# Moving the buffers of a transformer kernel to other addresses in the on-chip memory

## The chip, the cores and the metric

The kernel runs on one core of a Trainium2 chip. The metric is the device time of one execution in microseconds (us), as the median over runs. A core has a matrix engine (TensorE, PE in the rows below, with its weight loads shown apart as PEld), a vector engine (VectorE, DVE), a scalar engine (ScalarE, ACT), a general engine (GpSimd, POOL) and queues that start DMA transfers (SyncE, SP). All of them work on one on-chip memory (SBUF) of 128 partitions; an address in this text is a byte offset inside a partition, the same in all of them.

## The reference, cut to what matters

Two transformer blocks in float32 run one after the other over a sequence of 512 tokens of width 1024. Every block has two layers, and every layer is a mixer (causal pooling, dilated attention, or retention beside stick-breaking attention) and a gated feed-forward part of width 2816.

```python
h = _modulate(_rmsnorm(x, norm2_g[layer]), sh2, sc2)
a, v = jnp.split(h @ w_up, 2, axis=-1)          # 1024 x 5632
a = _causal_dwconv(a, conv_w, conv_b)
x = x + g2[:, None, :] * ((jax.nn.silu(a) * v) @ w_down)   # 2816 x 1024
...
h = rms_norm(x, norm2_g[l])
x = x + (jax.nn.silu(h @ w_gate[l]) * (h @ w_up[l])) @ w_down[l]
```

## The kernel before, in words

Activations are held transposed, 128 channels by 512 tokens to a chunk, and every float32 product is made from three products of a reduced format (fp32r): each operand is split in a high and a low part, and high x high, high x low and low x high are added up in PSUM. `three` (L435) issues these three matmuls, all through `mm` (L432, the call on L433). Each has 128x128 weights (512 bytes of a partition) and streams one chunk of 512 columns (2048 bytes of a partition) past them. A step of `gemm` (L441) does this for 8 or 11 chunks.

The weights come from one long array in DRAM, `stream`. `load` (L1781) of the SP queue brings a unit of one or two tiles, mostly 1 MB, into one of two buffers `RAW`, or, for the modulation weights of the first stages, into one of three buffers `AR`. ScalarE copies a tile from `RAW` to one of three buffers `WH`, which rounds it to the high half (`prep`, through L821). GpSimd (first 79 tiles, L1687) or VectorE (all others, L1234) subtracts that from `RAW` and writes the low half to one of three buffers `WL`. VectorE multiplies what is in `AR` with the condition vector (L1256).

The moving operands are pairs of a high and a low buffer. `H1H` and `H1L` hold the input of most projections. `PH`/`PL` (named H2Ha, H2La in the rows) hold the pooled values, `AH`/`AL` (H2Hb, H2Lb) the second input of the attention projections, `HH`/`HL` (H2Hc, H2Lc) the outputs of the second block's mixers, and `GH`/`GL` (GHa, GHb, GHd and GLa, GLb, GLd) the gated hidden values that the down projections read. `SPH`/`SPO` are a smaller pair, read with the weights `KR`.

There are 10,416 matmuls of 512 columns in fp32r: 6720 stream H1H or H1L, 48 H2Ha or H2La, 1152 H2Hb or H2Lb, 384 H2Hc or H2Lc, 1056 GHd or GLd, and 528 each GHa/GLa and GHb/GLb. The rest of the matrix engine's work is in plain float32 (norm sums, transposes, attention products).

All buffers are placed by hand: `at(name, offset, n)` in `Core.__init__` (L257) gives a buffer of n words its byte offset. Different stages put different buffers over the same bytes. Each matmul of `gemm` starts at a multiple of 512 bytes inside its weight buffer and a multiple of 2048 bytes inside its moving buffer, so the remainder of a buffer's offset by 256 is that of every operand read from it. Before the change this remainder is 128 for H1H, H1L, RAW, WH, WL, SS and SG, and 64 for the H2, GH and GL pairs, SPH, SPO, KR, Q, K, AA, OC, W and AR.

Of the kernel before, what the change touches and what calls it, by code (L numbers as in the profile page):

```python
# [7 lines left out]
F32R = mybir.dt.float32r  # L8
# [7 lines left out]
SLOT = 2048  # L16
WSLOT = HC * 128
# [76 lines left out]
NCOL = 0  # L94
# [154 lines left out]
class Core:  # L249


    def __init__(self, nc, stream, cd, colsd, xt, basd, attd, retd, out):
# [4 lines left out]
        def at(name, offset, n, dt=F32):  # L257
            return nc.alloc_sbuf_tensor_at(name, [128, n], dt, offset=offset)


        self.XT = at("XT", 1152, 4096)
        self.H1H, self.H1L = at("H1H", 17536, 4096, F32R), at("H1L", 33920, 4096, F32R)
        self.RAW = [at(f"RAW{i}", 50304 + 8192 * i, SLOT) for i in range(2)]
        self.WH = [at(f"WH{i}", 66688 + 5632 * i, WSLOT, F32R) for i in range(3)]
        self.WL = [at(f"WL{i}", 83584 + 5632 * i, WSLOT, F32R) for i in range(3)]
        self.SS, self.SG = at("SS", 100480, 512), at("SG", 102528, 512)
        self.CO = at("CO", 104576, NCOL)
        self.MOD, self.AB, self.KON = at("MOD", 106176, 112), at("AB", 106624, 40), at("KON", 106784, 2)
        self.BAS, self.ONE128 = at("BAS", 106816, 576), at("ONES", 109120, 128)
        self.PS = [nc.alloc_psum_tensor(f"PS{i}", [128, 512], F32) for i in range(8)]  # L270

        self.AR = [at("AR0", 109632, SLOT), at("AR1", 117824, SLOT), at("AR2", 126016, SLOT)]
        self.COND = at("COND", 134208, 1024)
        early = {"SQ": [at(f"SQ{i}a", 138304 + 2048 * i, 512) for i in range(2)], "R": at("Ra", 142400, 512),
                 "T": [at(f"T{i}a", 144448 + 2048 * i, 512) for i in range(3)],
                 "V": [at(f"V{i}a", 150592 + 2048 * i, 512) for i in range(4)]}
        self.PH, self.PL = at("H2Ha", 158784, 4096, F32R), at("H2La", 175168, 4096, F32R)
        self.PU = [at(f"U{i}", 191552 + 2112 * i, 528) for i in range(2)]
        self.PV = [[at(f"V{j}{i}", 195776 + 4224 * i + 2112 * j, 528) for j in range(2)] for i in range(2)]

        self.AH, self.AL = at("H2Hb", 109632, 4096, F32R), at("H2Lb", 126016, 4096, F32R)
        self.ATT = at("ATT", 142400, 1152)
        self.QT = [at(f"QT{i}", 147008 + 6144 * i, 1536) for i in range(2)]
        self.KT = [at(f"KT{i}", 159296 + 6144 * i, 1536) for i in range(2)]
        self.VV = [at(f"VV{i}", 171584 + 6144 * i, 1536) for i in range(2)]
        self.OT, self.VF, self.STAT = at("OT", 183872, 4096), at("VF", 200256, 512), at("STAT", 202304, 16)
        self.AT = [at(f"T{i}b", 208512 + 2048 * i, 512) for i in range(3)]
        self.AV = [at(f"V{i}b", 214656 + 2048 * i, 512) for i in range(4)]
        self.SB = [at("SB0", 202368, 1536), at("SB1", 208512, 1536)]
        self.PT = [at("PT0", 214656, 1536), at("PT1", 220800, 1536)]  # L290

        late = {"SQ": [at(f"SQ{i}q", 109632 + 2048 * i, 512) for i in range(2)], "R": at("Rc", 113728, 512),
                "T": [at(f"T{i}c", 115776 + 2048 * i, 512) for i in range(3)],
                "V": [at(f"V{i}c", 121920 + 2048 * i, 512) for i in range(4)]}
# [5 lines left out]
        self.Y = [[at(f"Ya{i}", 203840 + 2048 * i, 512) for i in range(2)],  # L300
                  [at(f"Yb{i}", 175168 + 2048 * i, 512) for i in range(2)]]
        self.SI = [[at(f"SIa{i}", 207936 + 2048 * i, 512) for i in range(2)],
                   [at(f"SIb{i}", 179264 + 2048 * i, 512) for i in range(2)]]
        gh, gl = at("GHd", 113728, 5632, F32R), at("GLd", 136256, 5632, F32R)
        si = [at(f"SId{i}", 162880 + 2048 * i, 512) for i in range(2)]
        self.GH += [gh, gh]
        self.GL += [gl, gl]
        self.SI += [si, si]

        self.HH, self.HL = at("H2Hc", 113728, 4096, F32R), at("H2Lc", 130112, 4096, F32R)  # L310
        self.RT = at("RT", 146496, 3072)
        self.Q = [at(f"Q{i}", 158784 + 2048 * i, 512) for i in range(3)]
        self.K = [at(f"K{i}", 164928 + 2048 * i, 512) for i in range(3)]
        self.G = [at(f"G{i}", 171072 + 2048 * i, 512) for i in range(2)]
        self.W = [at(f"W{i}", 175168 + 2048 * i, 512) for i in range(3)]
        self.VR = at("VR", 181312, 512)
        self.TMP = {"k": at("TMP0", 183360, 512), "q": at("TMP1", 185408, 512)}
        self.AA, self.SPL = at("AA", 187456, 1280), at("SPL", 192576, 1280)
        self.SPH, self.SPO = at("SPH", 197696, 1280, F32R), at("SPO", 202816, 1280, F32R)
        self.KR = at("KR", 207936, 256, F32R)  # L320
        self.OB = [at(f"OB{i}", 208960 + 2048 * i, 512) for i in range(2)]
        self.OC = [at(f"OC{i}", 213056 + 2048 * i, 512) for i in range(2)]

        self.ONES = self.ONE128[:, :]
        self.IDENT, self.STRICT, self.MEANS = self.BAS[:, 0:128], self.BAS[:, 384:512], self.BAS[:, 512:576]
# [1529 lines left out]
```

How the kernel before makes its waits and increments, by code:

```python
    def wait_ge(self, sem, value):  # L243
        if value > self.met.get(id(sem), 0):
            self.engine.wait_ge(sem, value)
            self.met[id(sem)] = value
# [181 lines left out]
    def vacate(b):  # L428
        if b in free:
            q.wait_ge(*free[b])
# [10 lines left out]
    def gemm(t, H, L, ready, freed, mid=None):  # L441
        b, n = BANK[t], UNITS[TILES[t][0]][2][TILES[t][1]][3]
        q.wait_ge(*c.low(t))
        vacate(b)
        for k in range(n):
            if mid and k in (2, 4):
                mid(k)
            if ready:
                q.wait_ge(*ready(k))
            ins = three(b, t, 128 * k, chunk(H, k), chunk(L, k), k == 0, k == n - 1)
        ins.then_inc(c.mm, 1)
        free[b] = freed
# [1 line left out]
    def group(t0, inputs, freed, order=tuple(range(8)), split=4, hook=None):  # L455
        for n, k in enumerate(order[:split]):
            for x in range(3):
                H, L, ready = inputs[x]
                if n == 0:
                    q.wait_ge(*c.low(t0 + x))
                    vacate(BANK[t0 + x])
                q.wait_ge(*ready(k))
                three(BANK[t0 + x], t0 + x, 128 * k, chunk(H, k), chunk(L, k), n == 0, False)
                if hook:
                    hook(3 * n + x)
        for x in range(3):
            H, L, ready = inputs[x]
            for k in order[split:]:
                q.wait_ge(*ready(k))
                ins = three(BANK[t0 + x], t0 + x, 128 * k, chunk(H, k), chunk(L, k), False, k == order[-1])
            ins.then_inc(c.mm, 1)
            free[BANK[t0 + x]] = freed[x]
```

## Time and profile before

| what | value |
|---|---|
| median of 3 runs | 2838.7 us (2837.08 to 2839.62) |
| profiled execution | 2840.38 us, of which its span 2838.6 us |
| PE busy | 2723.9 us (96% of the span) |
| DVE, ACT, POOL busy | 1523.9, 1062.1, 388.6 us |
| granted TensorE clock, mean | 0.984 |
| DMA | 297.19 MB, mean 105 GB/s |

The span runs from the first to the last instruction of the core; what lies around it is 1.8 us here. Busy time of PE counts a stretch in which matmuls overlap once, so a busy PE is not a PE at its peak; how far apart two matmuls start is read from the rows of the timeline.

### The profile page before, as it was taken

The page shows a single profiled execution, that of the slowest core. Times are in us where ns is not written, and L with a number is a line of the kernel's source. Part 1 is how long each engine was busy: PE and PEld are TensorE (multiplying, and loading weights), DVE is VectorE, ACT ScalarE, POOL GpSimd, SP SyncE. Part 2 cuts the span into 40 slices and gives each one's busy share as a digit, 9 for nine tenths or more (in the row PEclk, how much of TensorE's full clock was granted, in tenths as well). Part 3 has the DMA queues.
Part 4 walks back from the last instruction along what each step waited for, and adds up shares of the span by engine and source line. Part 5 has one row for each costly group of instructions (what it writes and reads, how often), then busy time and mean ns, then how long its engine had stood idle before and what let it go on. Part 6 is the DMA issues. An engine that isn't in the chain of part 4 may idle for free.

```text
span 2838.6 us, 30758 instructions
## 1 busy us (share of the span) xinstructions
PE 2723.9 (96%) x12742; PEld 2186.1 (77%) x12742; DVE 1523.9 (54%) x2035; ACT 1062.1 (37%) x1488; POOL 388.6 (14%) x196
## 2 busy tenths in 40 slices
PE   5689999989999999899999999999999999999998
PEld 3568888778888887688888777788887777788886
DVE  7888857655555555654345555443344455443343
ACT  3333233344444444343234455422223455422231
POOL 3444545410000000000000001010010011010010
PEclk9799999999999999999999999999999999999999
DMA  7354645321212111122222221222223212223222
GB/s 271 119 210 183 248 177 198 135 83 60 75 61 74 69 66 60 60 89 101 95 89 102 97 75 60 76 102 97 89 95 113 90 60 75 76 103 101 85 100 71
DMA packets 45690, 297.19 MB, mean 105 GB/s; under 512 B 4976, under 2 KB 5104, under 8 KB 16368
## 3 DMA queue, kind: packets, MB, share of 16 engines
q1 hardware_dynamic: 45408, 294.71, 28.6%
q8 instruction: 101, 1.65, 0.2%
q10 hardware_dynamic: 144, 0.52, 0.1%
q14 instruction: 37, 0.30, 0.0%
HBM read 293.12 MB, written 2.10 MB: 104 GB/s over the span
## 4 chain that ended last, share of the span: by engine, by line
PE 89%; DVE 3%; ACT 1%; issue 1%; POOL 0%; DVEq 0%; ACTq 0%; POOLq 0%
PE PS L433 87%; PE PS L478 2%; DVE XT L1237 0%; DVE H2Lb L1234 0%; DVE WL L1234 0%; ACT H1H L821 0%; DVE AA L1234 0%; DVE H1L L1234 0%; DVE AR L1256 0%; ACT WH L821 0%; DVE T0c L1234 0%; DVE T1a L1234 0%; DVE T1c L1234 0%; ACT AA L821 0%; DVE T0a L1234 0%
## 5 line engine op out<-in xcount | busy, mean ns | idle before, releaser
L433 PE MATMUL PS<-H1H,WH 128*128 128x512 f32 x2240 | 898.2, 401 | 39.0 <-DVE H1L L1234 32.5
L433 PE MATMUL PS<-H1H,WL 128*128 128x512 f32 x2240 | 878.6, 392 | 0.0
L433 PE MATMUL PS<-H1L,WH 128*128 128x512 f32 x2240 | 877.8, 392 | 0.0
L1234 DVE TENSOR_TENSOR WL<-RAW,WH 128x1024 fp32r<-128x1024 f32 (+1 forms) x330 | 435.2, 1320 | 381.4 <-ACT WH L821 380.5
L821 ACT ACTIVATE WH<-RAW 128x1024 fp32r<-128x1024 f32 (+2 forms) x409 | 449.9, 1102 | 268.5 <-PE PS L433 257.7
L433 PEld LDWEIGHTS PS<-H1H,WH 128*128 128x128 f32 x2240 | 424.2, 189 | 143.6 <-issue 44.7
L433 PEld LDWEIGHTS PS<-H1L,WH 128*128 128x128 f32 x2240 | 424.8, 190 | 90.5 <-issue 5.3
L433 PEld LDWEIGHTS PS<-H1H,WL 128*128 128x128 f32 x2240 | 423.9, 189 | 91.0
L1687 POOL TENSOR_TENSOR WL<-RAW,WH 128x1024 fp32r<-128x1024 f32 (+2 forms) x79 | 229.8, 2914 | 235.8 <-ACT WH L821 235.6
L1256 DVE CUSTOM_DVE_ANT_0 AR<-AR,COND,CO 128x1024 f32<-128x1024 f32 x112 | 237.3, 2161 | 0.4
L433 PE MATMUL PS<-H2Hb,WH 128*128 128x512 f32 x384 | 160.0, 417 | 11.5 <-DVE H2Lb L1234 11.5
L433 PE MATMUL PS<-H2Lb,WH 128*128 128x512 f32 x384 | 152.6, 397 | 0.0
L433 PE MATMUL PS<-H2Hb,WL 128*128 128x512 f32 x384 | 152.6, 397 | 0.0
L1687 POOL TENSOR_TENSOR SId<-SId,SG 128x512 f32<-128x512 f32 x44 | 57.3, 1302 | 668.5 <-ACT SId L821 668.5
L433 PE MATMUL PS<-GHd,WL 128*128 128x512 f32 x352 | 138.7, 394 | 0.0
L433 PE MATMUL PS<-GHd,WH 128*128 128x512 f32 x352 | 138.7, 394 | 0.0
L433 PE MATMUL PS<-GLd,WH 128*128 128x512 f32 x352 | 138.7, 394 | 0.0
L1687 POOL TENSOR_TENSOR TMP<-TMP,RT 128x512 f32<-128x512 f32 x16 | 20.7, 1294 | 772.6 <-ACT TMP L821 772.6
L821 ACT ACTIVATE SB<-SB,STAT 128x768 f32<-128x768 f32 x64 | 60.0, 938 | 125.7 <-DVE STAT L1485 124.6
L1234 DVE TENSOR_TENSOR XT<-PS,XT 128x512 f32<-128x512 f32 x48 | 33.1, 689 | 128.8 <-PE PS L433 128.7
L433 PEld LDWEIGHTS PS<-H2Hb,WH 128*128 128x128 f32 x384 | 72.7, 189 | 31.8 <-DVE H2Lb L1234 7.9
L821 ACT ACTIVATE GHd<-SId 128x512 fp32r<-128x512 f32 x44 | 27.8, 633 | 168.3 <-DVE SId L1234 168.3
(246 smaller groups left out, 3334.3 us busy)
## 6 DMA issues: line engine op xcount, KB each, us to landing
RAW<-stream SPq DMA_DIRECT2D x170, 1024.0 KB, 4.8
AR<-stream SPq DMA_DIRECT2D x56, 1024.0 KB, 6.9
RAW<-stream SPq DMA_DIRECT2D x64, 704.0 KB, 4.0
RT<-ret SPq DMA_DIRECT2D x2, 1536.0 KB, 6.3
RAW<-stream SPq DMA_DIRECT2D x4, 640.0 KB, 6.9
XT<-xt SPq DMA_DIRECT2D x2, 1024.0 KB, 8.9
y<-XT SPq DMA_DIRECT2D x8, 256.0 KB, 2.5
ATT<-att SPq DMA_DIRECT2D x1, 576.0 KB, 3.4
```

Source lines behind the costliest of these rows:

```text
L433: return nc.tensor.matmul(out, weights, moving, start=start, stop=stop, skip_group_check=True)
L478: ins = nc.tensor.transpose(PS[b][:, 128 * n:128 * n + 128], block, c.IDENT)
L821: return nc.scalar.activation(out, src, fn, **kw)
L1234: return nc.vector.tensor_tensor(out, a, b, op)
L1256: ins = nc.vector.tensor_tensor_reduce(src, src, c.COND[:, :], 1.0, bias, ALU.mult, ALU.add, c.mod(first + n, 1))
L1687: return nc.gpsimd.tensor_tensor(out, a, b, op)
```

## The change

The diff gives nearly every buffer another offset. No instruction, loop, wait or size is touched. After it the remainder by 256 is 0 for H1H, H1L, RAW, WH, WL, SS, SG and CO, for all H2, GH and GL pairs, SPH, SPO, KR, Q, K, W, AA, OB, OC and the buffers QT, KT and VV of the attention. It stays 64 for AR, COND, BAS and ONES (110400, the offset of AR0, is 431.25 x 256) and becomes 64 for SB and PT, and 128 for Yb and SIb. XT keeps its offset, with the remainder 128. MOD, AB and KON move down into the gap behind XT. Gaps of 256 or 512 bytes are left between some buffers, as between H1H and H1L.

```diff
         self.XT = at("XT", 1152, 4096)
-        self.H1H, self.H1L = at("H1H", 17536, 4096, F32R), at("H1L", 33920, 4096, F32R)
-        self.RAW = [at(f"RAW{i}", 50304 + 8192 * i, SLOT) for i in range(2)]
-        self.WH = [at(f"WH{i}", 66688 + 5632 * i, WSLOT, F32R) for i in range(3)]
-        self.WL = [at(f"WL{i}", 83584 + 5632 * i, WSLOT, F32R) for i in range(3)]
+        self.MOD, self.AB, self.KON = at("MOD", 17536, 112), at("AB", 17984, 40), at("KON", 18144, 2)
+        self.H1H, self.H1L = at("H1H", 18432, 4096, F32R), at("H1L", 35072, 4096, F32R)
+        self.RAW = [at(f"RAW{i}", 51456 + 8192 * i, SLOT) for i in range(2)]
+        self.WH = [at(f"WH{i}", 68096 + 5632 * i, WSLOT, F32R) for i in range(3)]
+        self.WL = [at(f"WL{i}", 84992 + 5632 * i, WSLOT, F32R) for i in range(3)]
...
-        self.AR = [at("AR0", 109632, SLOT), at("AR1", 117824, SLOT), at("AR2", 126016, SLOT)]
+        self.AR = [at(f"AR{i}", 110400 + 8192 * i, SLOT) for i in range(3)]
...
-        self.PH, self.PL = at("H2Ha", 158784, 4096, F32R), at("H2La", 175168, 4096, F32R)
+        self.PH, self.PL = at("H2Ha", 159744, 4096, F32R), at("H2La", 176128, 4096, F32R)
...
-        self.AH, self.AL = at("H2Hb", 109632, 4096, F32R), at("H2Lb", 126016, 4096, F32R)
+        self.AH, self.AL = at("H2Hb", 110592, 4096, F32R), at("H2Lb", 127488, 4096, F32R)
...
-        self.GH = [at("GHa", 158784, 5632, F32R), at("GHb", 130112, 5632, F32R)]
-        self.GL = [at("GLa", 181312, 5632, F32R), at("GLb", 152640, 5632, F32R)]
+        self.GH = [at("GHa", 160768, 5632, F32R), at("GHb", 131328, 5632, F32R)]
+        self.GL = [at("GLa", 183808, 5632, F32R), at("GLb", 153856, 5632, F32R)]
...
-        gh, gl = at("GHd", 113728, 5632, F32R), at("GLd", 136256, 5632, F32R)
+        gh, gl = at("GHd", 114688, 5632, F32R), at("GLd", 139264, 5632, F32R)
...
-        self.HH, self.HL = at("H2Hc", 113728, 4096, F32R), at("H2Lc", 130112, 4096, F32R)
+        self.HH, self.HL = at("H2Hc", 115456, 4096, F32R), at("H2Lc", 132096, 4096, F32R)
...
-        self.SPH, self.SPO = at("SPH", 197696, 1280, F32R), at("SPO", 202816, 1280, F32R)
-        self.KR = at("KR", 207936, 256, F32R)
+        self.SPH, self.SPO = at("SPH", 199680, 1280, F32R), at("SPO", 204800, 1280, F32R)
+        self.KR = at("KR", 209920, 256, F32R)
```

## Rows read from the trace of the kernel before

**Rows 1.** The page: busy time, and the chain that ended last.

```profile
PE 2723.9 (96%) x12742; PEld 2186.1 (77%) x12742; DVE 1523.9 (54%) x2035; ACT 1062.1 (37%) x1488; POOL 388.6 (14%) x196
...
PE 89%; DVE 3%; ACT 1%; issue 1%; POOL 0%; DVEq 0%; ACTq 0%; POOLq 0%
```

**Rows 2.** Windows: the head, the first feed-forward stage, its densest stretch, all after it.

```profile
core 0: us, PE busy (x) PEld busy (x) DVE busy (x) ACT busy (x) POOL busy (x), PEclk, DMA share, GB/s
...
300.00:350.00 50.00, 50.00 (x217) 40.32 (x216) 44.76 (x39) 13.09 (x12) 27.07 (x9) 1.00 0.72 270
0.00:200.00 200.00, 133.54 (x486) 101.33 (x486) 160.97 (x208) 64.86 (x84) 81.00 (x43) 0.87 0.51 200
200.00:556.00 356.00, 354.69 (x1543) 289.07 (x1543) 254.89 (x254) 114.63 (x136) 172.90 (x59) 1.00 0.52 195
...
1584.00:2838.60 1254.60, 1235.50 (x5368) 988.11 (x5366) 577.55 (x756) 469.60 (x658) 107.68 (x78) 0.99 0.24 85
```

**Rows 3.** Timeline of PE, H1H and H1L streamed: first and last of 55 matmuls.

```profile
start us, us, engine line op out<-in xcount [idle before <-releaser]
1299.75 0.39 PE L433 MATMUL PS<-H1H,WL 128*128 128x512 f32 x1
...
1311.99 0.39 PE L433 MATMUL PS<-H1H,WL 128*128 128x512 f32 x1
```

**Rows 4.** Timeline of PE, GHb and GLb streamed: first and last of 43 matmuls.

```profile
1503.04 0.39 PE L433 MATMUL PS<-GHb,WH 128*128 128x512 f32 x1
...
1512.84 0.39 PE L433 MATMUL PS<-GHb,WH 128*128 128x512 f32 x1
```

**Rows 5.** Timeline of PE, H2Hb and H2Lb streamed: first and last of 12 matmuls.

```profile
632.96 0.39 PE L433 MATMUL PS<-H2Hb,WH 128*128 128x512 f32 x1
...
635.53 0.40 PE L433 MATMUL PS<-H2Hb,WL 128*128 128x512 f32 x1
```

**Rows 6.** Timeline of PE at half clock, H1H and H1L: 7 matmuls.

```profile
26.68 0.63 PE L433 MATMUL PS<-H1L,WH 128*128 128x512 f32 x1
...
29.24 0.63 PE L433 MATMUL PS<-H1L,WH 128*128 128x512 f32 x1
```

**Rows 7.** Timeline of PE, plain float32: 8 matmuls, 2560 columns together, and the next.

```profile
1778.40 2.39 PE L433 MATMUL PS<-Q,K 128*128 128x512 f32 x8 [0.78 <-ACT OB L821]
1780.55 0.48 PE L433 MATMUL PS<-H2Hc,WH 128*128 128x512 f32 x1
```

**Rows 8.** Timeline of PE, SPH and SPO on KR: first of 8 (2560 columns), and the next.

```profile
1661.38 0.45 PE L433 MATMUL PS<-SPH,KR 128*128 128x512 f32 x1
...
1662.66 0.44 PE L433 MATMUL PS<-H1H,WH 128*128 128x512 f32 x1
```

**Rows 9.** Groups by line, PE, from 200 us on: one of each three kinds.

```profile
line engine op names shapes xcount | busy us, mean ns | idle before us <-releasers
L433 PE MATMUL PS<-H1H,WL 128*128 128x512 f32 x2097 | 819.7, 391 | 0.0
...
L433 PE MATMUL PS<-H2Lb,WH 128*128 128x512 f32 x384 | 152.6, 397 | 0.0
...
L433 PE MATMUL PS<-GHd,WL 128*128 128x512 f32 x352 | 138.7, 394 | 0.0
...
L433 PE MATMUL PS<-GHa,WL 128*128 128x512 f32 x176 | 69.3, 394 | 0.0
...
L433 PE MATMUL PS<-H2Hc,WH 128*128 128x512 f32 x128 | 53.1, 415 | 3.3 <-DVE WL L1234 2.0 <-DVE AA L1234 0.9
```

**Rows 10.** Waits of PE from 200 to 556 us.

```profile
PE PS L433 <- ACT SQ1a L821: 0.6, 1, 0.6
PE PS L433 <- POOL H1L L1687: 0.2, 1, 0.2
```

**Rows 11.** The page: the copy of a tile to WH with its waits, and the loads.

```profile
L821 ACT ACTIVATE WH<-RAW 128x1024 fp32r<-128x1024 f32 (+2 forms) x409 | 449.9, 1102 | 268.5 <-PE PS L433 257.7
...
RAW<-stream SPq DMA_DIRECT2D x170, 1024.0 KB, 4.8
```

More of the change, by code:

```diff
@@ L261, in __init__ @@
         self.XT = at("XT", 1152, 4096)
-        self.H1H, self.H1L = at("H1H", 17536, 4096, F32R), at("H1L", 33920, 4096, F32R)
-        self.RAW = [at(f"RAW{i}", 50304 + 8192 * i, SLOT) for i in range(2)]
-        self.WH = [at(f"WH{i}", 66688 + 5632 * i, WSLOT, F32R) for i in range(3)]
-        self.WL = [at(f"WL{i}", 83584 + 5632 * i, WSLOT, F32R) for i in range(3)]
-        self.SS, self.SG = at("SS", 100480, 512), at("SG", 102528, 512)
-        self.CO = at("CO", 104576, NCOL)
-        self.MOD, self.AB, self.KON = at("MOD", 106176, 112), at("AB", 106624, 40), at("KON", 106784, 2)
@@ L269, in __init__ @@
-        self.BAS, self.ONE128 = at("BAS", 106816, 576), at("ONES", 109120, 128)
-        self.PS = [nc.alloc_psum_tensor(f"PS{i}", [128, 512], F32) for i in range(8)]
-        self.AR = [at("AR0", 109632, SLOT), at("AR1", 117824, SLOT), at("AR2", 126016, SLOT)]
[L273 to L276, printed above, removed]
@@ L277, in __init__ @@
-        self.PH, self.PL = at("H2Ha", 158784, 4096, F32R), at("H2La", 175168, 4096, F32R)
-        self.PU = [at(f"U{i}", 191552 + 2112 * i, 528) for i in range(2)]
-        self.PV = [[at(f"V{j}{i}", 195776 + 4224 * i + 2112 * j, 528) for j in range(2)] for i in range(2)]
-        self.AH, self.AL = at("H2Hb", 109632, 4096, F32R), at("H2Lb", 126016, 4096, F32R)
-        self.ATT = at("ATT", 142400, 1152)
-        self.QT = [at(f"QT{i}", 147008 + 6144 * i, 1536) for i in range(2)]
-        self.KT = [at(f"KT{i}", 159296 + 6144 * i, 1536) for i in range(2)]
@@ L285, in __init__ @@
[L285 to L294, printed above, removed]
@@ L296, in __init__ @@
-        self.NORM = [early] * 3 + [late] * 6
-        self.GH = [at("GHa", 158784, 5632, F32R), at("GHb", 130112, 5632, F32R)]
-        self.GL = [at("GLa", 181312, 5632, F32R), at("GLb", 152640, 5632, F32R)]
[L300 to L303, printed above, removed]
@@ L304, in __init__ @@
-        gh, gl = at("GHd", 113728, 5632, F32R), at("GLd", 136256, 5632, F32R)
-        si = [at(f"SId{i}", 162880 + 2048 * i, 512) for i in range(2)]
+        self.MOD, self.AB, self.KON = at("MOD", 17536, 112), at("AB", 17984, 40), at("KON", 18144, 2)
+        self.H1H, self.H1L = at("H1H", 18432, 4096, F32R), at("H1L", 35072, 4096, F32R)
+        self.RAW = [at(f"RAW{i}", 51456 + 8192 * i, SLOT) for i in range(2)]
+        self.WH = [at(f"WH{i}", 68096 + 5632 * i, WSLOT, F32R) for i in range(3)]
@@ new lines, in __init__ @@
+        self.WL = [at(f"WL{i}", 84992 + 5632 * i, WSLOT, F32R) for i in range(3)]
+        self.SS, self.SG = at("SS", 101888, 512), at("SG", 103936, 512)
+        self.CO = at("CO", 105984, NCOL)
+        self.BAS, self.ONE128 = at("BAS", 107584, 576), at("ONES", 109888, 128)
+        self.PS = [nc.alloc_psum_tensor(f"PS{i}", [128, 512], F32) for i in range(8)]
+        self.AR = [at(f"AR{i}", 110400 + 8192 * i, SLOT) for i in range(3)]
+        self.COND = at("COND", 134976, 1024)
+        early = {"SQ": [at(f"SQ{i}a", 139072 + 2048 * i, 512) for i in range(2)], "R": at("Ra", 143168, 512),
+                 "T": [at(f"T{i}a", 145216 + 2048 * i, 512) for i in range(3)],
+                 "V": [at(f"V{i}a", 151360 + 2048 * i, 512) for i in range(4)]}
@@ new lines, in __init__ @@
+        self.PH, self.PL = at("H2Ha", 159744, 4096, F32R), at("H2La", 176128, 4096, F32R)
+        self.PU = [at(f"U{i}", 192512 + 2112 * i, 528) for i in range(2)]
+        self.PV = [[at(f"V{j}{i}", 196736 + 4224 * i + 2112 * j, 528) for j in range(2)] for i in range(2)]
+        self.AH, self.AL = at("H2Hb", 110592, 4096, F32R), at("H2Lb", 127488, 4096, F32R)
+        self.ATT = at("ATT", 143872, 1152)
+        self.QT = [at(f"QT{i}", 148480 + 6144 * i, 1536) for i in range(2)]
+        self.KT = [at(f"KT{i}", 160768 + 6144 * i, 1536) for i in range(2)]
@@ new lines, in __init__ @@
+        self.VV = [at(f"VV{i}", 173056 + 6144 * i, 1536) for i in range(2)]
+        self.OT, self.VF, self.STAT = at("OT", 185344, 4096), at("VF", 201728, 512), at("STAT", 203776, 16)
+        self.AT = [at(f"T{i}b", 209984 + 2048 * i, 512) for i in range(3)]
+        self.AV = [at(f"V{i}b", 216128 + 2048 * i, 512) for i in range(4)]
+        self.SB = [at("SB0", 203840, 1536), at("SB1", 209984, 1536)]
+        self.PT = [at("PT0", 216128, 1536), at("PT1", 222272, 1536)]
+        late = {"SQ": [at(f"SQ{i}q", 110592 + 2048 * i, 512) for i in range(2)], "R": at("Rc", 114688, 512),
+                "T": [at(f"T{i}c", 116736 + 2048 * i, 512) for i in range(3)],
+                "V": [at(f"V{i}c", 122880 + 2048 * i, 512) for i in range(4)]}
@@ new lines, in __init__ @@
+        self.NORM = [early] * 3 + [late] * 6
+        self.GH = [at("GHa", 160768, 5632, F32R), at("GHb", 131328, 5632, F32R)]
+        self.GL = [at("GLa", 183808, 5632, F32R), at("GLb", 153856, 5632, F32R)]
+        self.Y = [[at(f"Ya{i}", 206336 + 2048 * i, 512) for i in range(2)],
+                  [at(f"Yb{i}", 176512 + 2048 * i, 512) for i in range(2)]]
+        self.SI = [[at(f"SIa{i}", 210432 + 2048 * i, 512) for i in range(2)],
+                   [at(f"SIb{i}", 180608 + 2048 * i, 512) for i in range(2)]]
@@ L306, in __init__ @@
+        gh, gl = at("GHd", 114688, 5632, F32R), at("GLd", 139264, 5632, F32R)
+        si = [at(f"SId{i}", 161792 + 2048 * i, 512) for i in range(2)]
         self.GH += [gh, gh]
@@ L308, in __init__ @@
         self.SI += [si, si]
-        self.HH, self.HL = at("H2Hc", 113728, 4096, F32R), at("H2Lc", 130112, 4096, F32R)
[L311 to L318, printed above, removed]
-        self.SPH, self.SPO = at("SPH", 197696, 1280, F32R), at("SPO", 202816, 1280, F32R)
-        self.KR = at("KR", 207936, 256, F32R)
-        self.OB = [at(f"OB{i}", 208960 + 2048 * i, 512) for i in range(2)]
-        self.OC = [at(f"OC{i}", 213056 + 2048 * i, 512) for i in range(2)]
+        self.HH, self.HL = at("H2Hc", 115456, 4096, F32R), at("H2Lc", 132096, 4096, F32R)
+        self.RT = at("RT", 148480, 3072)
+        self.Q = [at(f"Q{i}", 160768 + 2048 * i, 512) for i in range(3)]
+        self.K = [at(f"K{i}", 166912 + 2048 * i, 512) for i in range(3)]
+        self.G = [at(f"G{i}", 173056 + 2048 * i, 512) for i in range(2)]
+        self.W = [at(f"W{i}", 177152 + 2048 * i, 512) for i in range(3)]
+        self.VR = at("VR", 183296, 512)
+        self.TMP = {"k": at("TMP0", 185344, 512), "q": at("TMP1", 187392, 512)}
+        self.AA, self.SPL = at("AA", 189440, 1280), at("SPL", 194560, 1280)
+        self.SPH, self.SPO = at("SPH", 199680, 1280, F32R), at("SPO", 204800, 1280, F32R)
+        self.KR = at("KR", 209920, 256, F32R)
+        self.OB = [at(f"OB{i}", 210944 + 2048 * i, 512) for i in range(2)]
+        self.OC = [at(f"OC{i}", 215040 + 2048 * i, 512) for i in range(2)]
         self.ONES = self.ONE128[:, :]
```

## The prediction

> **What bounds the kernel now.** I read the page's busy times and chain first. The matrix engine is busy 96% of the span and makes up 89% of the chain that ended last [rows 1]. The windows say where: until 200 us it is busy 133.5 of 200 us, at a mean clock of 0.87, while VectorE is busy 161; from 200 to 556 us it is busy 354.7 of 356 [rows 2] and waits 0.8 us in all [rows 10]; from 1584 us it is busy 98.5%. So from 200 us on the time is the number of matmuls times the distance between their starts, and a change of addresses matters if it alters that distance. In the head it would be worth little, since VectorE sets the pace there.
>
> Next I read that distance in the timeline, and this is what decides. The rows print 0.01 us, so I divide long stretches. With H1H and H1L streamed, 54 distances take 12.24 us, 226.7 ns each [rows 3]. With GHb and GLb, 42 take 9.80 us, 233.3 ns [rows 4]. With H2Hb and H2Lb, 11 take 2.57 us, 233.6 ns [rows 5], which I take as 233.3. The shape, the weight buffers and the full clock are the same. At half clock, 1.2 GHz, 6 distances with H1H take 2.56 us, 426.7 ns [rows 6]: 512 columns at one a cycle and nothing more. At full clock, 2.4 GHz, the columns alone would take 213.3 ns. So at full clock each matmul carries an excess, 13.3 ns over H1 and 20.0 over the others.
>
> What differs between the two? Not the stage: H1 and H2Hb tiles alternate within the attention stage. Not the distance between high and low buffer: it is 16384 bytes for H1 and for H2Hb both. What differs is the offset's remainder by 256, 128 for H1 and 64 for all others. The excess looks like an effect of address, of a kind that shows only when operands are read at full rate.
>
> **The change part by part.** No instruction, wait or transfer is added or removed; every cost is in what an access takes at its new address.
>
> *The matmuls.* The two excesses are 32 and 48 columns' time, and (256 - remainder)/4 is 32 and 48: as if the reader went to the end of the 256-byte block in which an operand ends, and began the next only then. At remainder 0 the operand ends with its block and this excess is gone. What is left then is a fixed cost per matmul, which plain float32 shows because its slower rate hides the other part: 8 matmuls with 2560 columns take 2.15 us against 2.133 us at 1.2 columns a ns, 2.1 ns each [rows 7]. I take 213.3 + 2.1 = 215.4 ns. The bounds for the distance at remainder 0: from below 213.3 ns, the columns alone; from above 240.0 ns, if 0 counts as a whole block more (64 columns, the line 233.3, 226.7 carried one step the wrong way). I take the lower side, since it needs no extra read.
>
> The counts from 200 us on, where each kind of row stands for three of equal count: 3 x 2097 = 6291 over H1, and 3 x (384 + 352 + 176 + 176 + 128) = 3648 over the others [rows 9]; the second 176 is GHb, whose three rows equal GHa's.
> - H1: 6291 x (226.7 - 215.4 = 11.3 ns) = 71.1 us
> - others: 3648 x (233.3 - 215.4 = 17.9 ns) = 65.3 us
> - SPH and SPO: 8 matmuls over 2560 columns take 1.28 us where the columns are 1.07 us [rows 8]. There are 160; even 12 ns each is 2 us, and I count 1.
> - Taken off: the stretches at half clock after 200 us, where the excess is already hidden. The clock of 0.99 to 1.00 there [rows 2] leaves by estimate 60 matmuls, 1 us.
>
> *The rest of the load on the other engines.* With a matrix engine 6% faster the others must keep up. The tightest place is 300 to 350 us: VectorE 44.8, POOL 27.1 of 50 us, DMA share 0.72 [rows 2]. Six percent more makes that 47.5, 28.7 and 0.76. VectorE has 2.5 us in 50 left; the cover is thin, and over the whole 356 us it has 101 us to spare. I charge 2 us for new waits; if VectorE held half of that gain in this stage it would be 10 us. After 556 us VectorE is busy below 55%.
>
> *The streamed buffers.* A load of 1 MB lands in 4.8 us, and one unit of two tiles is needed per 48 x 0.227 = 10.9 us; ScalarE's copy to WH waits mostly for the matrix engine (257.7 of 268.5 us) [rows 11]. Faster or slower landing is worth nothing while this slack of 6 us stands. AR stays at remainder 64, so VectorE's multiplication, which sets the head, changes nothing: 0, at most 3 us either way. For ScalarE, VectorE and GpSimd I have no row that tells addresses apart, and outside the head they hide under matmuls: 0.
>
> *Sum.* 71.1 + 65.3 + 1 - 1 - 2 = 134 us. Against this execution, 2838.6 + 1.8 us around the span = 2840.4, that gives 2706; it stands 1.7 us above the median, so against the median 2838.7 - 134 = **2705 us**.
>
> *A rule on the other side.* The trace shows 426.7 ns at half and 226.7 or 233.3 ns at full clock, all with operands that start at multiples of 64 bytes [rows 3, 4, 6]. The Trainium skill, SBUF — State Buffer, section Specifications (TRN2), gives the memory lines of 16 bytes, with full bandwidth for an access that stays in a line; by that grain all these operands were aligned before, and the sum would be 0. The two distances differ all the same, so this trace doesn't bear the 16-byte grain out as the only one.
>
> **The rivals.**
> - *Only the step from 64 to 128 bytes counts* (a grain of 128 bytes, or only the place of the moving operand against its weights, which is equal for H1 before and for all after). Then 13.3 ns stay, say as the price of the weight load beside the stream, and the others fall to 226.7: 3648 x 6.67 ns = 24 us, 2814 us. For it: each remainder is seen once, and weights always at 128. Against: with both at 64, SPH and SPO on KR show (1.28 - 1.07)/8 = 27 ns each, more than 13.3 [rows 8], though these change bank often and the number is rough.
> - *A step of 64 bytes at each level.* 233.3, 226.7 and then 220.0 (6.67 ns is 16 columns, 64 bytes). 6291 x 6.67 + 3648 x 13.3 ns = 42 + 49 = 91 us, 2748 us. It also covers a smaller part of the excess left by weight loads.
> - *Remainder 0 is the worst, not the best.* If a block is read beyond the end also when the operand ends on it, the distance is 240.0: 6291 x 13.3 + 3648 x 6.67 ns = 84 + 24 = 108 us more, 2947 us. It decides as soon as the distance over H1 is above 226.7 by more than the others fall below 233.3 (in the ratio 3648 to 6291, 0.58). For it: the pattern alone, 48 then 32, doesn't tell 0 from 64. Against: it makes the even address dearer than any other.
> - *The map does nothing.* Something that I haven't seen sets the two distances, and the time stays at 2839. Against: the three GH pairs, at other places and in other stages, all show 394 ns for the length of a matmul without an interruption, and H1 391 [rows 9]; and the alternation of H1 and H2Hb in one stage excludes most other causes.
>
> On the weight load the Trainium skill, TensorE: Matmul & The Clock Gate, section Step-by-step, says that the engine has two independent read ports, so that loading the next weights takes nothing from the running matmul. No run here shows it; it speaks against the first rival's way to keep 13.3 ns. The same page, Back-to-back issue gap, has N/2.4 + 2.5 ns without a term for the address, 215.8 ns for 512 columns; the trace's 226.7 and 233.3 disagree with it.
>
> **How the numbers follow.** The full effect, near 2705: 0.47. The 64-byte step, near 2748: 0.12. Only 64 to 128, near 2814: 0.20. Nothing: 0.08. Worst at 0, near 2947: 0.10, and 0.03 for a slowdown by another way. The forecast's own range goes from 2838.7 - (6291 x 13.3 + 3648 x 20.0 ns = 157 us) = 2682 to about 2720, with 10 us of new waits and some distances that don't settle. The range for 8 in 10 starts at 2678 (the 157 us, and up to 4 more from the head and from SPH and SPO) and takes in the first two rivals up to 2822. Within 0.2% of the time before, about 6 us, is what a measurement of this kernel can't tell from no change. Faster 0.79, same 0.08, slower 0.13.
>
> **What would show it.** In the timeline the distance over H1H and over GHb becomes the same, 215 to 216 ns, and the mean of the uninterrupted kinds falls by as much as the distance. The distance at half clock stays 426.7. 200 to 556 us shrinks by some 5%, the head stays near 200 us, and VectorE's busy time is unchanged. The prediction is wrong if H1's distance stays at 226.7 or rises, or if waits of the matrix engine for VectorE appear between 200 and 556 us.

## The result, and the profile after

| | median, us | runs | ratio to before (95% interval) | span of the profiled execution, us |
|---|---|---|---|---|
| before | 2839.16 | 2837.08 to 2840.28 (4) | | 2838.6 |
| after | 2819.19 | 2819.10 to 2819.76 (4) | 0.9931 (0.9914 to 0.9948) | 2817.4 |

The new map is faster by 20 us, 0.7%. The forecast had 134 us; the range held the time only because it took in the first rival (2814 us), and that is the one which came true in size.

The page of the kernel after, busy times, answers to [rows 1]: PE lost 19.9 us of busy time with the same 12742 matmuls, and DVE and ACT lost under 1 us each.

```profile
PE 2704.0 (96%) x12742; PEld 2188.8 (78%) x12742; DVE 1523.1 (54%) x2035; ACT 1061.6 (38%) x1488; POOL 386.6 (14%) x196
...
RAW<-stream SPq DMA_DIRECT2D x170, 1024.0 KB, 4.7
```

The windows of after, same stretches as [rows 2] (columns there):

```profile
0.00:200.00 200.00, 134.80 (x490) 102.72 (x491) 162.22 (x210) 64.84 (x85) 81.73 (x43) 0.87 0.51 200
200.00:556.00 356.00, 350.37 (x1541) 288.89 (x1540) 257.83 (x258) 118.37 (x141) 172.19 (x60) 1.00 0.52 195
300.00:350.00 50.00, 50.00 (x223) 41.39 (x222) 46.17 (x41) 11.95 (x11) 27.44 (x9) 1.00 0.78 288
```

Clock and head are as before. From 300 to 350 us PE starts 223 matmuls where it started 217, and still waits for nobody. From 200 to 556 us it is idle for 5.6 us: 5.0 of them is one wait for DVE behind the stage, which comes before 556 us now; before, the same wait of 5.1 us came just after 556 us.

Now the distance between starts, PE's timeline of after. First H1H and H1L streamed (first and last of 70 matmuls), then GHb and GLb (76), then SPH and SPO on KR with the next matmul behind them:

```profile
1296.05 0.39 PE L433 MATMUL PS<-H1H,WL 128*128 128x512 f32 x1
...
1311.69 0.39 PE L433 MATMUL PS<-H1H,WL 128*128 128x512 f32 x1
...
1492.80 0.39 PE L433 MATMUL PS<-GHb,WH 128*128 128x512 f32 x1
...
1509.80 0.39 PE L433 MATMUL PS<-GHb,WH 128*128 128x512 f32 x1
...
1649.31 0.45 PE L433 MATMUL PS<-SPH,KR 128*128 128x512 f32 x1
1649.60 0.39 PE L433 MATMUL PS<-SPO,KR 128*128 128x512 f32 x1
...
1650.48 0.27 PE L433 MATMUL PS<-SPO,KR 128*128 128x128 f32 x1
1650.59 0.45 PE L433 MATMUL PS<-H1H,WH 128*128 128x512 f32 x1
```

69 distances over H1 take 15.64 us, 226.7 ns, exactly what [rows 3] had. 75 over GHb take 17.00 us, 226.7 ns, where [rows 4] had 233.3. SPH and SPO take 1.28 us as before [rows 8]; 0.29 of it is the first of the eight distances and 0.11 the last, and the six between, 1920 columns, take 0.88 us, 13.3 ns each above their columns. So H1 gained nothing and the others 6.67 ns each. The groups by line of after, from 200 us on, say the same of every matmul, against [rows 9]:

```profile
L433 PE MATMUL PS<-H1H,WL 128*128 128x512 f32 x2096 | 818.8, 391 | 0.0
L433 PE MATMUL PS<-H2Hb,WL 128*128 128x512 f32 x384 | 151.5, 395 | 0.0
...
L433 PE MATMUL PS<-GHd,WL 128*128 128x512 f32 x352 | 136.9, 389 | 0.0
...
L433 PE MATMUL PS<-GHa,WL 128*128 128x512 f32 x176 | 68.5, 389 | 0.0
...
L433 PE MATMUL PS<-H2Hc,WH 128*128 128x512 f32 x128 | 52.6, 411 | 3.5 <-DVE WL L1234 2.1 <-DVE AA L1234 1.0 <-DVE H2Lc L1234 0.5
```

H1 stays at 391 ns, GHd and GHa fall from 394 to 389, H2 by 2 to 4.

**Where the 21.2 us of span went.** I measured each stage between the starts of its first matmul and of the next stage's, in both traces. The eight down projections, 264 matmuls each over GH and GL, went from 61.6 to 59.8 us: 1.76 us, which is 264 x 6.67 ns, and 14.1 in all. The attention stage went from 638.9 to 635.2 us (3.75), the two mixers lost 1.05 us each, the head 1.2 (not traced further); the stages that stream H1 alone are within 0.05 us. Together 21.2. Attention gave half of its 1152 x 6.67 ns = 7.7 us, because there H2 is streamed in short stretches. In after a stretch doesn't begin at 226.7. PE's timeline, H2Hb behind an interruption, up to the next one:

```profile
637.79 0.48 PE L433 MATMUL PS<-H2Hb,WH 128*128 128x512 f32 x1
638.11 0.39 PE L433 MATMUL PS<-H2Lb,WH 128*128 128x512 f32 x1
...
639.04 0.40 PE L433 MATMUL PS<-H2Hb,WL 128*128 128x512 f32 x1
639.28 0.60 PE L478 MATMUL PS<-BAS,SB 128*128 128x128 f32 x4
```

From 638.11 to 639.04 four distances take 0.93 us, 232 ns. Farther on in a long stretch it is 226 (from 627.84 to 629.65 us, 8 distances).

The mean over all stretches of the trace that begin with H2Hb (88 of them, fewer reach the later places) shows how it settles: 232.7, 231.9, 230.2 and 229.6 ns for the first four distances of after, 227.0 for the tenth. In the trace of before, with the other addresses, the same stretches stay between 232.6 and 234.0 over the first ten. H1 settles in the same way in both traces. So at the start of a stretch the old and the new address cost nearly the same, and the 6.67 ns are saved only once the stream has run on for about ten matmuls.

### The profile page after: what moved, and what is told of

It is laid out like the page before. It is cut to its first block, busy times and chain, and to the rows that moved or that the text cites. A ratio compares the mean times of both kernels' runs of the same rounds, so it can differ in the third digit from the quotient of the medians.

```text
span 2817.4 us, 30758 instructions
## 1 busy us (share of the span) xinstructions
PE 2704.0 (96%) x12742; PEld 2188.8 (78%) x12742; DVE 1523.1 (54%) x2035; ACT 1061.6 (38%) x1488; POOL 386.6 (14%) x196
## 4 chain that ended last, share of the span: by engine, by line
PE 89%; DVE 3%; ACT 1%; issue 1%; DVEq 0%; POOL 0%; ACTq 0%; POOLq 0%
PE PS L433 87%; PE PS L478 2%; DVE H2Lb L1234 0%; DVE XT L1237 0%; DVE WL L1234 0%; DVE AA L1234 0%; ACT H1H L821 0%; DVE AR L1256 0%; DVE H1L L1234 0%; ACT WH L821 0%; DVE T1b L1234 0%; DVE T0c L1234 0%; DVE T1c L1234 0%; ACT AA L821 0%; ACT OC L821 0%
## 5 line engine op out<-in xcount | busy, mean ns | idle before, releaser
L1687 POOL TENSOR_TENSOR WL<-RAW,WH 128x1024 fp32r<-128x1024 f32 (+2 forms) x79 | 229.6, 2912 | 232.5 <-ACT WH L821 232.3
```

Source lines behind the costliest of these rows:

```text
L1687: return nc.gpsimd.tensor_tensor(out, a, b, op)
```

## The experiments

Two questions: does the remainder of an operand's own address count, or its place against the other operand's, and what are the 13.3 ns that stayed? Below, the *place* is the moving operand's offset less that of its weights, modulo 256 bytes, written from -96 to 128. Before it was 0 for H1 (128 and 128) and -64 for the others (64 and 128); for SPH and SPO on KR it was 0 as well (64 and 64). After it is 0 for all. That 256 bytes is the period and not 512 can be read from after: GHb and GLb lie 256 bytes off their weights modulo 512, GHa and GLa 0, and both take 226.7 ns.

**1. Shift only the upper part of the old map by 64 bytes.** Made from the kernel before, so that GH and H2 lie at remainder 128 with the weights; H1, RAW, WH and WL stay where they were, at 128.

```diff
-            return nc.alloc_sbuf_tensor_at(name, [128, n], dt, offset=offset)
+            return nc.alloc_sbuf_tensor_at(name, [128, n], dt, offset=offset + (64 if offset >= 109632 else 0))
```

> The kernel before with one part of the change alone: every buffer from 109632 on (H2, GH and GL pairs, AR, all stage buffers) moved up by 64 bytes, to the remainder 128, which H1, RAW, WH and WL already had. Relative theory (the distance between matmul starts hangs on the moving operand's remainder by 256 minus the weights'; equal gives 226.7 ns): all pairs fall from 233.3 to 226.7 ns, and the time is that of the changed kernel, about 2819 us. Grain theory (the moving operand wants a multiple of 128 bytes, whatever the weights have): the same, 2819. Theory that multiples of 256 bytes are needed, or that the streamed buffers' own alignment brought the gain: 2835 to 2839, as before.

Measured: 2818.64 us (2815.62 to 2820.05), ratio 0.9924 (0.9909 to 0.9939). The timeline and the groups from 200 us on:

```profile
1330.18 0.39 PE L433 MATMUL PS<-GHb,WL 128*128 128x512 f32 x1
...
1339.93 0.39 PE L433 MATMUL PS<-GHb,WH 128*128 128x512 f32 x1
...
L433 PE MATMUL PS<-GHd,WL 128*128 128x512 f32 x352 | 136.9, 389 | 0.0
```

43 distances take 9.75 us, 226.7 ns. One shift of 64 bytes has the whole gain. That H1, RAW and the weights go from remainder 128 to 0 adds nothing that these runs tell.

**2. Move only the weights of the new map.** Everything else at remainder 0, the weights at 64, 128 and 192.

```diff
-        self.WH = [at(f"WH{i}", 68096 + 5632 * i, WSLOT, F32R) for i in range(3)]
-        self.WL = [at(f"WL{i}", 84992 + 5632 * i, WSLOT, F32R) for i in range(3)]
+        # w64: 67904 and 84800; w128: 67968 and 84864; w192: 68032 and 84928
+        self.WH = [at(f"WH{i}", 67904 + 5632 * i, WSLOT, F32R) for i in range(3)]
+        self.WL = [at(f"WL{i}", 84800 + 5632 * i, WSLOT, F32R) for i in range(3)]
```

> The changed kernel with WH and WL moved down by 192 bytes to the remainder 64; all moving operands stay at 0. Relative theory: moving minus weights is -64 (192), as it was for GH and H2 before, so every one of the 9939 matmuls after 200 us goes from 226.7 to 233.3 ns, H1's too: 66 us more, 2885 us. Grain theory, or any in which only the moving operand's own address counts: no change, 226.7 ns and 2819 us.

> The changed kernel with WH and WL moved down by 128 bytes to the remainder 128; all moving operands at 0, so moving minus weights is 128. Relative theory: the distance is another than 226.7 ns; if each 64 bytes is worth 6.7 ns in one direction (-64 cost 6.7 more, so +64 gives 6.7 less), it is 213.3 to 215.4 or 240.0, thus about 2705 or 2950 us. Grain theory and own-address theories: 226.7 ns, 2819 us.

> The changed kernel with WH and WL moved down by 64 bytes to the remainder 192; moving minus weights is +64. Relative theory: if the effect has a direction, 220.0 ns and 2753 us; if it counts only how far apart they are, 233.3 ns as for -64, 2885 us. Grain theory and own-address theories: 226.7 ns, 2819 us.

| weights at | place | median, us | ratio to before (95% interval) | distance, ns |
|---|---|---|---|---|
| 64 | -64 | 2877.62 | 1.0132 (1.0115 to 1.0149) | 233.3 |
| 128 | 128 | 2869.73 | 1.0106 (1.0091 to 1.0121) | 233.4 |
| 192 | 64 | 2835.92 | 0.9988 (0.9978 to 0.9997) | 228.8 |

The timeline with the weights at 64 (first and last of 43 matmuls), and its group of H1; then the timeline with them at 128 (45) and at 192 (44):

```profile
1330.20 0.39 PE L433 MATMUL PS<-H1H,WH 128*128 128x512 f32 x1
...
1340.00 0.39 PE L433 MATMUL PS<-GHb,WH 128*128 128x512 f32 x1
...
L433 PE MATMUL PS<-H1H,WL 128*128 128x512 f32 x2098 | 830.6, 396 | 0.0
```

```profile
1329.68 0.40 PE L433 MATMUL PS<-H1H,WH 128*128 128x512 f32 x1
...
1339.95 0.40 PE L433 MATMUL PS<-GHb,WL 128*128 128x512 f32 x1
```

```profile
1330.03 0.39 PE L433 MATMUL PS<-GHb,WH 128*128 128x512 f32 x1
...
1339.87 0.39 PE L433 MATMUL PS<-GLb,WH 128*128 128x512 f32 x1
```

42 distances in 9.80 us are 233.3 ns, 44 in 10.27 are 233.4, 43 in 9.84 are 228.8. H1 never moved from 0 in these kernels and went from 391 to 396 ns a matmul: the moving operand's own remainder doesn't make its price. The weights' own remainder doesn't either, since at 128 they cost nothing in experiment 1 and 6.67 ns here. With the weights at 64, the old price now falls on H1 as well, 6291 x 6.67 = 42 us, against 38.5 measured over the kernel before. Between the weights at 64 and at 128 lie 8 us that the distances explain only in part: at 128 the last two down projections take 232.3 ns a matmul, the others 233.3.

**3. Three places in one kernel.** The three weight buffers take turns, each at its own remainder.

```diff
-        self.WH = [at(f"WH{i}", 68096 + 5632 * i, WSLOT, F32R) for i in range(3)]
-        self.WL = [at(f"WL{i}", 84992 + 5632 * i, WSLOT, F32R) for i in range(3)]
+        self.WH = [at(f"WH{i}", 67840 + 11264 * i + [32, 96, 160][i], WSLOT, F32R) for i in range(3)]
+        self.WL = [at(f"WL{i}", 73472 + 11264 * i + [32, 96, 160][i], WSLOT, F32R) for i in range(3)]
+        # mixb: [32, 192, 224] in both lines
```

> The changed kernel with the three pairs of weight buffers at the remainders 32, 96 and 160 (tiles 0, 1, 2 of every three), so moving minus weights is -32, -96 and +96; the distance is read tile by tile. Known from before and the runs so far: 0 gives 226.7 ns, -64 233.3, 128 233.4, +64 229.2. Smooth curve: -32 about 230, -96 about 233, +96 about 231, and no remainder below 226.7. [...] Time by the smooth curve: mean 231.3, 2819 + 9939 x 4.7 ns = 2865 us.

> The changed kernel with the three pairs of weight buffers at the remainders 32, 192 and 224, so moving minus weights is -32, +64 and +32. -32 must repeat what the run with 32, 96 and 160 shows and +64 the 229.2 ns of the run with all weights at 192. Smooth curve with its best place at 0: +32 about 228. If the best place lies between 0 and +64, +32 is below 226.7 ns, and all weights there would beat the changed kernel. Time about 2819 + 9939 x 1.7 ns = 2836 us by the smooth curve.

One run each: 2880.06 us (before, on that chip, 2840.28) and 2862.97 us. A tile of the down projection is 33 matmuls on one buffer. The boundaries of three in mixa, weights at 160 (place 96), 32 (-32), 96 (-96):

```profile
1336.97 0.40 PE L433 MATMUL PS<-GHb,WH 128*128 128x512 f32 x1
...
1344.67 0.40 PE L433 MATMUL PS<-GHb,WH 128*128 128x512 f32 x1
...
1352.38 0.39 PE L433 MATMUL PS<-GHb,WH 128*128 128x512 f32 x1
...
1360.10 0.40 PE L433 MATMUL PS<-GHb,WH 128*128 128x512 f32 x1
```

7.70, 7.71 and 7.72 us, so 233.3, 233.6 and 233.9 ns. In mixb the same reading gives 233.3 at 32, 233.3 at -32 and 229.1 at 64. A step of 64 bytes at each level would have given more than two values in order; instead there is 226.7 at 0, 229 at 64 and one plateau.

**4. Places under 64 bytes.** H1H and H1L moved up by 16 bytes, GHa and GLa down by 16, GHd and GLd up by 4. RAW and SId, which one of the copies reads, went up by 32.

```diff
-        self.H1H, self.H1L = at("H1H", 18432, 4096, F32R), at("H1L", 35072, 4096, F32R)
+        self.H1H, self.H1L = at("H1H", 18432, 4104, F32R)[:, 4:4100], at("H1L", 35072, 4104, F32R)[:, 4:4100]
...
-        self.GH = [at("GHa", 160768, 5632, F32R), at("GHb", 131328, 5632, F32R)]
-        self.GL = [at("GLa", 183808, 5632, F32R), at("GLb", 153856, 5632, F32R)]
+        self.GH = [at("GHa", 160736, 5640, F32R)[:, 4:5636], at("GHb", 131328, 5632, F32R)]
+        self.GL = [at("GLa", 183776, 5640, F32R)[:, 4:5636], at("GLb", 153856, 5632, F32R)]
...
-        gh, gl = at("GHd", 114688, 5632, F32R), at("GLd", 139264, 5632, F32R)
+        gh, gl = at("GHd", 114688, 5640, F32R)[:, 1:5633], at("GLd", 139264, 5640, F32R)[:, 1:5633]
```

> The changed kernel with small offsets of the moving operands against weights at 0: H1H and H1L +16 bytes, GHa and GLa -16, GHd and GLd +4, all others unchanged (so GHb and GLb must repeat 226.7 ns). The runs so far have 0 at 226.7, +64 at 229.1 and -32, +32, +96, 128 and -96 between 233.2 and 233.8. If what counts is that both lie on the same place within 256 bytes to the byte: +16, -16 and +4 are all near 233.3, 2819 + (6291 + 528 + 1056) x 6.7 ns = 2872 us. If the grain is 32 bytes: those that stay in the same 32 bytes as 0 (+16, +4) keep 226.7, or cost by the straddling alone. If the best place is near 0 but not at it, one of them is below 226.7.

One run: 2860.68 us (before 2839.01). Its groups from 200 us on, and the first and last matmul of the two down projections over GHa, 264 matmuls each:

```profile
L433 PE MATMUL PS<-H1H,WL 128*128 128x512 f32 x2096 | 828.0, 395 | 0.0
...
L433 PE MATMUL PS<-GHd,WL 128*128 128x512 f32 x344 | 137.8, 401 | 0.0
...
L433 PE MATMUL PS<-GHa,WL 128*128 128x512 f32 x176 | 69.9, 397 | 0.0
```

```profile
310.81 0.39 PE L433 MATMUL PS<-GHa,WH 128*128 128x512 f32 x1
...
373.02 0.40 PE L433 MATMUL PS<-GHa,WL 128*128 128x512 f32 x1
...
495.57 0.39 PE L433 MATMUL PS<-GHa,WH 128*128 128x512 f32 x1
...
556.94 0.39 PE L433 MATMUL PS<-GHa,WL 128*128 128x512 f32 x1
```

A length of 389 to 391 ns was 226.7 ns of distance, 396 was 233.3. Here 16 bytes up is 395 (231.6 in the timeline), 4 up 401, the worst of all (about 238). 16 down is 397, which is a mean of two values: 263 distances take 62.21 us in the first projection, 236.5 ns, and 61.37 in the second, 233.3, with the same buffers at the same place. So off place 0 the place alone doesn't fix the distance to the nanosecond. At place 0 all eight projections of after have 226.7, and no place tried beats it:

| place, bytes | -96 | -64 | -32 | -16 | 0 | 4 | 16 | 32 | 64 | 96 | 128 |
|---|---|---|---|---|---|---|---|---|---|---|---|
| distance, ns | 233.9 | 233.3 | 233.3 | 233.3 and 236.5 | 226.7 | 238 | 231.6 | 233.3 | 229 | 233.3 | 233.4 |

**5. What are the 13.3 ns: a smaller load.** If they are the weight load's reads, loading half as many weight columns must cut them. The two correction matmuls take 64 columns of their weights, and fill 64 rows of PSUM: the other 64 rows miss their correction.

```diff
-        mm(PS[b][:, :], wh, lo, False, False)
-        return mm(PS[b][:, :], wl, hi, False, last)
+        mm(PS[b][0:64, :], wh[:, 0:64], lo, False, False)
+        return mm(PS[b][0:64, :], wl[:, 0:64], hi, False, last)
```

> The changed kernel, but the two correction matmuls of every three (high weights by low input, low weights by high input) use only the first 64 of the 128 weight columns, so half of the outputs lack the corrections; it still streams 512 columns three times. Weight-load theory (the 13.3 ns that stay at full clock are the price of loading 128 columns of weights beside the stream): in two of three distances the load beside is half as long, 6.7 ns less each, triple mean 222.2 ns, 2775 us. Fixed-cost theory (13.3 ns belong to a 512-column fp32r stream whatever is loaded): 226.7 ns throughout, 2819 us.

> As the run with 64 weight columns in the correction matmuls, and WH and WL at the remainder 64 (moving minus weights -64). Weight-load theory: the whole 20 ns scale with the load, 10 in two of three distances, mean 226.7 ns, 2819 us. If only the placement part (6.7 ns) scales: 213.3 + 13.3 + 4.4 = 231 ns, 2863 us. If nothing scales: 233.3 ns, 2878 us.

2840.72 us with the weights at 0 and 2861.46 with them at 64, one run each (before, beside them, 2840.28). Neither theory: the smaller load made the kernel 21 us slower than after. Timeline, weights at 0, first and last of seven:

```profile
1330.11 0.39 PE L433 MATMUL PS<-GHb,WH 128*128 128x512 f32 x1
1330.33 0.39 PE L433 MATMUL PS<-GLb,WH 128*64 128x512 f32 x1
...
1331.48 0.39 PE L433 MATMUL PS<-GHb,WH 128*128 128x512 f32 x1
```

Six distances take 1.37 us, 228 ns, over longer stretches 229.5; the best place has lost part of its advantage. With the weights at 64 the mean is 231.6, less than 233.3, but not everywhere: the two projections over GHa stay at 233.3, the six over GHb and GHd go to 231.1, all at the same place. So the price isn't the load's width times a constant. That it depends on when, or over what length, the load's reads lie under the stream is argued, not shown: these matmuls also fill only half of their outputs.

**6. Fixed, or per column?** Each matmul split into two of 256 columns, each with its own weight load: twice as many matmuls, the same columns.

```diff
-        mm(PS[b][:, :], wh, hi, first, False)
-        mm(PS[b][:, :], wh, lo, False, False)
-        return mm(PS[b][:, :], wl, hi, False, last)
+        for n, (weights, moving) in enumerate(((wh, hi), (wh, lo), (wl, hi))):
+            for x in (0, 256):
+                ins = mm(PS[b][:, x:x + 256], weights, moving[:, x:x + 256], first and n + x == 0, last and n == 2)
+        return ins
```

> The changed kernel with every fp32r matmul of 512 columns issued as two of 256; the computation is the same, with twice as many weight loads. It asks what the 13.3 ns are that stay at full clock (226.7 against 213.3 ns). Fixed cost per matmul: 256 columns take 106.7 + 13.3 = 120 ns, 240 per 512 columns, 9939 x 13.3 ns = 132 us more, 2951 us. Cost per column streamed: 113.3 ns, no change, 2819 us. Weight load beside the stream: there are twice as many loads, as the fixed cost, or more, since a load has half as long to hide.

2940.72 us, in one run (before 2839.01). Timeline, two matmuls to a row:

```profile
1329.36 0.40 PE L433 MATMUL PS<-H1L,WH 128*128 128x256 f32 x2
...
1330.80 0.40 PE L433 MATMUL PS<-H1L,WH 128*128 128x256 f32 x2
```

12 distances take 1.44 us, 120.0 ns each: 106.7 for 256 columns, plus the same 13.3. It is a price per matmul with its load, not per column, as the six short distances of SPH and SPO also have it. The whole kernel pays 121.5 us over after, where 9939 x 13.3 ns would be 132.

**7. Another type.** First the two corrections alone took the upper halves of the same words as bfloat16 (their products are coarser).

```diff
+        def top(ap):
+            return ap.bitcast(mybir.dt.bfloat16).rearrange("p (n two) -> p n two", two=2)[:, :, 1]
...
-        mm(PS[b][:, :], wh, lo, False, False)
-        return mm(PS[b][:, :], wl, hi, False, last)
+        mm(PS[b][:, :], top(wh), top(lo), False, False)
+        return mm(PS[b][:, :], top(wl), top(hi), False, last)
```

> The changed kernel, but the two correction matmuls of every three read only the upper 16 bits of their float32 words, as bfloat16 with a step of 4 bytes, so the corrections are less precise; columns, addresses and footprint are the same, and half of the bytes count. If the 13.3 ns belong to reading 4-byte words at full rate, those two run at 216 ns and only the fp32r one keeps 226.7, mean 219, 2819 - 9939 x 7.6 ns = 2743 us. If they belong to the footprint or to the matmul as such: 226.7 ns, 2819 us.

2883.83 us in one run (before 2839.01). It doesn't answer its question, because the changes of type have a price of their own. Timeline:

```profile
1329.65 0.59 PE L433 MATMUL PS<-H1H,WH 128*128 128x512 f32 x1
1330.08 0.40 PE L433 MATMUL PS<-H1L,WH 128*128 128x512 bf16 x1
1330.32 0.39 PE L433 MATMUL PS<-H1H,WL 128*128 128x512 bf16 x1
1330.35 0.60 PE L433 MATMUL PS<-H1H,WH 128*128 128x512 f32 x1
```

The three starts lie 430, 240 and 30 ns apart, 700 for the triple, where three of one type take 680. So all three matmuls became bfloat16 (all products coarser), with the weight buffers at places 0, -64 and 64:

> The changed kernel with all three matmuls of every chunk reading only the upper 16 bits of their float32 words, as bfloat16 with a step of 4 bytes (coarser products, no change of data type between them), and with the three pairs of weight buffers at the remainders 0, 64 and 192, so moving minus weights is 0, -64 and +64 from tile to tile. If both the fixed 13.3 ns and the price of placement belong to fp32r: about 216 ns (213.3 and some 2 ns) in all three kinds of tile, 2819 - 9939 x 11 ns = 2710 us. If the fixed part is of any matmul with 512 columns from 4-byte steps: 226.7. If placement counts here too: tiles with the weights at 64 take longer than those at 0.

2797.8 us in one run (before 2840.63). The timeline at the boundaries of tiles of 33, with places 64, 0 and -64, and the weight loads' group:

```profile
1300.31 0.39 PE L433 MATMUL PS<-GHb,WH 128*128 128x512 bf16 x1
...
1307.75 0.39 PE L433 MATMUL PS<-GHb,WH 128*128 128x512 bf16 x1
...
1315.17 0.39 PE L433 MATMUL PS<-GHb,WH 128*128 128x512 bf16 x1
...
1322.65 0.39 PE L433 MATMUL PS<-GHb,WH 128*128 128x512 bf16 x1
...
L433 PEld LDWEIGHTS PS<-H1L,WH 128*128 128x128 bf16 x2240 | 217.8, 97 | 284.9 <-issue 13.6
```

7.44, 7.42 and 7.48 us: 225.5, 224.8 and 226.7 ns. The load lasts 97 ns instead of 190, and the distance at place 0 falls by under 2. So 11.5 ns of excess stay with another type and with a load half as long; neither float32r nor the length of the load makes up most of the 13.3. The spread over these three places is 1.9 ns where float32r has 6.67.

## Why the prediction was right in direction and wrong in size

**Right.** The matrix engine sets the time from 200 us on, through the distance between starts, and only its addresses matter. The two distances 226.7 and 233.3 are an effect of address: one shift of 64 bytes turns one into the other. At half clock it stays hidden, 426.7 ns after as before. The landing of RAW (4.7 for 4.8 us) and the busy times of DVE and ACT hardly moved, and the head by 1.2 us. The 2 us for new waits weren't needed: the one wait for DVE between 200 and 556 us is the 5 us that before had just behind them. The prediction's own first sign of being wrong came: H1's distance stayed at 226.7 ns.

**The step that failed** is this one: "At remainder 0 the operand ends with its block and this excess is gone. What is left then is a fixed cost per matmul, which plain float32 shows because its slower rate hides the other part". I had read both excesses, 13.3 and 20.0 ns, as one effect with two sizes, because (256 - remainder)/4 happens to be 32 and 48 columns. That was two points and a formula made for them, with the weights at one and the same remainder in both. They are two effects. 13.3 ns are paid per matmul whatever the map is: at 512 columns and at 256, with both operands at remainder 128 (before, experiment 1) or at 0 (after). The other 6.67 ns depend on the place of the moving operand against its weights. Plain float32's 2.1 ns, taken as what is fixed, were no measure of it: that row runs at 1.2 columns a ns, the rate of half clock, at which nothing of the excess shows in float32r either (426.7 ns).

Term by term: H1, forecast 71.1 us, measured 0, since its place was 0 before and after. The others, forecast 65.3 (3648 x 17.9 ns), measured 19.95 in the stages (14.1 + 3.75 + 2.1): 6.67 ns each in the down projections, about half of that in attention, where short stretches don't settle. "Some distances that don't settle" stood in the prediction's range, but at no price. SPH and SPO, forecast 1, measured 0.

**The rivals.** The first had two versions. Its "place of the moving operand against its weights" is what happened; its 24 us were 4 too many for attention and the mixers. Its other version, a grain of 128 bytes, falls with experiment 2: with the weights at 64 or 128 and the moving operand at 0 the distance is 233.3 or 233.4. My objection to it, 27 ns a matmul for SPH and SPO at equal remainders [rows 8], fell too: their place was 0 before and after and the 1.28 us stayed, and 0.13 of the 0.21 us of excess sit in the first and the last of the eight distances, while the six between have the same 13.3 ns. What makes those two longer isn't shown. The 64-byte step, the worst-at-0 and the does-nothing case are out by after's 226.7 over both. The 16-byte grain of the Trainium skill (SBUF — State Buffer, Specifications (TRN2)) doesn't tell these distances apart: at places that are multiples of 16 they run from 226.7 to 236.5 ns. The prediction's inference that loading the next weights takes nothing from the running matmul doesn't hold as it stands either: with narrower loads, in experiment 5, the distance changed at both places.

On the 13.3 ns that stayed, the Trainium skill, TensorE: Matmul & The Clock Gate, Back-to-back issue gap, has 2.5 ns beside the columns for the isolated gap, and about 131 ns a matmul of 512 columns for a stream of load and matmul pairs. The runs here agree with neither: such pairs have 13.3 ns beside the columns at 512 and at 256 columns in float32r, and 11.5 in bfloat16 with a 4-byte step.

**Open.** Why the place counts isn't shown. That the load of the next weights and the stream get in each other's way in the memory would fit: the effect goes by the difference of addresses, is absent at half clock, and changes when the load gets shorter (experiments 5 and 7). But that is argued only. The table isn't symmetric (64 is cheap, -64 isn't), the same place gave two distances (-16 in experiment 4, -64 with the narrow loads), and a stretch needs about ten matmuls to settle; none of this is explained. Nor is it settled what the fixed 13.3 ns consist of. A matmul that keeps the weights of the one before wasn't tried, and would be the next run.

## What to carry to other kernels

Where the matrix engine is saturated with float32r matmuls that each load their own weights, look at the distance between starts at full clock, and keep moving operand and weights at the same offset modulo 256 bytes. Expect the saving in long uninterrupted streams alone, and about half of it where the streams are as short as in the attention stage here. Which remainder it is, and how the DMA's and the other engines' buffers lie, made no difference between the remainders tried here (0, 64 and 128). Don't let a formula through two points carry a forecast: list which quantities were constant in both (here the weights' address), and give the formula that leaves them out no more than its rival. A price that a slower rate hides can't be read from a row at that slower rate.

## What the runs showed of the hardware that I had not expected

- The place makes up to 5% of the distance, 226.7 against 238 ns, and being off by 4 bytes is dearer than by 64.
- A narrower weight load (135 ns instead of 188) made the matmuls slower at the best place, 229.5 for 226.7 ns, and faster at a bad one, 231.6 for 233.3.
- After an interruption the stream takes about ten matmuls to come down to 226.7 ns (232.7 for the first distance in attention, 227.0 for the tenth); at place -64 it stays near 233.3 from the first.
- A change between float32r and bfloat16 from one matmul to the next makes the triple 20 ns longer than three of one type.
